# A two-layer decoder trunk on one core: in 17 groups of each mixed pass the fourth gathered row is summed on VectorE

## What is computed

```python
for layer in range(DEPTH):                       # 2
    h = rms_norm(x, norm_mix[layer])
    z = h @ w_in[layer]                          # 1024 x 2564
    ...
    mixed = jnp.concatenate([fox_o, dil_o, diff_o, s5_o], axis=-1)
    x = x + mixed @ w_out[layer]
    x = x + peer(rms_norm(x, norm_ffn[layer]), peer_wq[layer], peer_keys[layer],
                 peer_u[layer], peer_v[layer])
...
def chunk(xc):                                   # peer, 128 tokens
    ...
    ug = u_tab[ids]                              # ids: 128 tokens x 8 x 16
    act = gelu(einsum('td,thkd->thk', xc, ug)) * gate
    vg = v_tab[ids]
    return einsum('thk,thkd->td', act, vg)
```

## Time and profile before

| | before |
|---|---|
| median of 3 runs | 1836.35 us (1835.11 to 1844.07) |
| the profiled execution's own time | 1842.02 us |
| its span, first to last instruction | 1839.1 us |
| mean granted clock of PE | 0.905 of full speed |
| busy: PE / PEld | 1493.1 us (81%) / 799.9 us (43%) |
| busy: DVE / ACT / POOL | 1157.0 us (63%) / 389.9 us (21%) / 1082.8 us (59%) |
| moved by DMA | 649.87 MB, 353 GB/s on average |
| chain that ended last | PE 41%, DVE 32%, DMA 13%, issue 8%, POOL 4% |

### The profile page before, as it was taken

One profiled execution on the slowest core, in us unless ns is written; L12 is line 12 of the kernel. 1 busy time (PEld: TensorE's weight loads), 2 busy tenths in 40 slices (PEclk: granted clock), 3 DMA queues, 4 the chain that ended last, 5 costly groups with the idle time before them and its releaser, 6 DMA issues.

```text
span 1839.1 us, 15963 instructions
## 1 busy us (share of the span) xinstructions
PE 1493.1 (81%) x4780; PEld 799.9 (43%) x4780; DVE 1157.0 (63%) x2646; ACT 389.9 (21%) x991; POOL 1082.8 (59%) x1028
## 2 busy tenths in 40 slices
PE   6758379889898589889998579879998778777777
PEld 3546235445474234445464234445455433232332
DVE  6644954867469943877468933876648965445453
ACT  2221012233221121233221111233221121111111
POOL 0000345767666655777666655666766667777774
PEclk9768789989998889988999889999998988999889
DMA  7415589989999999999999999999999989999997
GB/s 307 160 35 207 204 359 380 399 297 363 373 401 408 340 418 409 405 369 385 374 401 408 336 415 351 395 340 331 374 376 405 369 301 410 409 409 409 407 388 307
DMA packets 179053, 649.87 MB, mean 353 GB/s; under 512 B 17783, under 2 KB 19319, under 8 KB 174105
## 3 DMA queue, kind: packets, MB, share of 16 engines
q0 software_dynamic: 147456, 536.94, 76.0%
q1 hardware_dynamic: 31512, 111.92, 15.7%
HBM read 644.07 MB, written 4.72 MB: 353 GB/s over the span
## 4 chain that ended last, share of the span: by engine, by line
PE 41%; DVE 32%; DMA 13%; issue 8%; POOL 4%; ACT 2%; DVEq 0%; SPq 0%; POOLq 0%
PE ps L1112 21%; DVE junk L865 12%; DMA ring_u<-table_u,ids 11%; PE ps L934 8%; PE ps L1069 3%; POOL ring_v L1143 2%; PE ps L1082 2%; DMA ring_v<-table_v,ids 1%; PE ps L999 1%; POOL ring_u L1138 1%; DVE W L690 1%; DVE W L842 1%; DVE W L844 1%; DVE W L845 1%; PE ps L1009 1%
## 5 line engine op out<-in xcount | busy, mean ns | idle before, releaser
L1112 PE MATMUL ps<-ring_v,diag 128*128 128x512 f32 x2048 | 982.4, 636 | 229.2 <-ACT diag L480 227.6
L865 DVE CUSTOM_DVE_ANT_0 junk<-ring_u,h 128x1024 bf16<-128x1024 f32 x512 | 627.4, 1225 | 268.1 <-DMA ring_u<-table_u,ids 212.5
L1138 POOL DMA_INDIRECT ring_u<-table_u,ids x512 | 536.1, 1047 | 387.7 <-DVE ids L849 204.9
L1143 POOL DMA_INDIRECT ring_v<-table_v,ids x512 | 546.5, 1067 | 352.2 <-PE ps L1112 269.9
L1112 PEld LDWEIGHTS ps<-ring_v,diag 128*128 128x128 f32 x2048 | 412.0, 205 | 761.4 <-issue 751.6
L471 ACT ACTIVATE acts<-dots 128x4 f32<-128x4 f32 x128 | 26.3, 205 | 998.6 <-DVE dots L865 998.6
L480 ACT ACTIVATE diag<-cst,weights 128x128 f32<-128x128 f32 x512 | 163.5, 390 | 39.2 <-DVE weights L874 39.0
L934 PE MATMUL ps<-W,hT 128*128 128x384 f32 (+2 forms) x384 | 142.9, 531 | 4.0 <-DVE hT L576 2.6
L1082 PE MATMUL ps<-hT,W 128*128 128x128 f32 x1024 | 117.7, 276 | 2.7 <-DVE hT L576 2.6
L1082 PEld LDWEIGHTS ps<-hT,W 128*128 128x128 f32 x1024 | 116.0, 192 | 3.8 <-DVE hT L576 3.8
L934 PEld LDWEIGHTS ps<-W,hT 128*128 128x128 f32 x384 | 73.7, 193 | 72.3 <-issue 36.9
(11 more groups left out here) (247 smaller groups left out, 1050.4 us busy)
## 6 DMA issues: line engine op xcount, KB each, us to landing
W<-w_in SPq DMA_DIRECT2D x32, 1282.0 KB, 15.2
W<-peer_wq SPq DMA_DIRECT2D x16, 2048.0 KB, 21.0
W<-w_out SPq DMA_DIRECT2D x4, 4096.0 KB, 19.5
ring_u<-table_u,ids POOLq DMA_INDIRECT x512, 7.8
ring_v<-table_v,ids POOLq DMA_INDIRECT x512, 7.7
W<-keys_t SPq DMA_DIRECT2D x4, 1024.0 KB, 8.3
zkv<-gain_mix SPq DMA_DIRECT2D x4, 512.0 KB, 16.0
toep<-ring_u SPq DMA_DIRECT2D x1, 2048.0 KB, 7.4
```

The costliest lines, as they stand in the source:

```text
L865: v.tensor_tensor_reduce(junk[:, :], ring_u[:, s, :], h[:, b, :], 1.0, 0.0, ALU.mult, ALU.add, dots[:, s:s + 1]).then_inc(dots_done, 1)
L1112: mm = pe.matmul(ps[:, c, :], diag[:, s, :], ring_v[:, s, c * 512:(c + 1) * 512], start=False, stop=False, skip_group_check=True)
L1138: gp.indirect_dma_start(ring_u[:, k % RING, :], None, table_u, bass.IndirectOffsetOnAxis(ap=ids[:, b, k:k + 1], axis=0)).then_inc(u_in[k % ...
L1143: gp.indirect_dma_start(ring_v[:, k % RING, :], None, table_v, bass.IndirectOffsetOnAxis(ap=ids[:, b, k:k + 1], axis=0)).then_inc(v_in[k % ...
```

## The change

`summed_on_vector(n, k)` picks slots: the fourth slot of a group, in the groups 1 to 5 and 8 to 19 of the passes 0 to 2, 51 slots in all. For those, DVE multiplies the v rows with the slot's weights and adds them to x, right behind the weights and ahead of the group's piece of the preparation; ACT writes no diagonal and PE makes no product for them, and the v gather that reuses such a slot waits for DVE instead of PE. The product with zeros at a pass's start is left out (the first product of a pass starts the sum), and the one with the identity at its end too; `gathered` now adds the PSUM sum to x instead of copying.

```diff
+def summed_on_vector(n, k):
+
+    i = k // RING_G
+    return n + 1 < PASSES and k % RING_G == RING_G - 1 and (1 <= i <= 5 or 8 <= i <= 19)
+
+def tensor_sums(t):
+
+    return sum(not summed_on_vector(k // SLOTS, k % SLOTS) for k in range(t))
...
@@ scalar, weigh
-                    a.wait_ge(v_used, RING_G * (m - 1))
-                for s in range(g * RING_G, (g + 1) * RING_G):
-                    a.activation(diag[:, s, :], ident, ACT.Copy, scale=weights[:, s:s + 1]).then_inc(diag_ready, 1)
+                    a.wait_ge(v_used, tensor_sums(RING_G * (m - 1)))
+                for j in range(RING_G):
+                    s = g * RING_G + j
+                    if not summed_on_vector(n, RING_G * i + j):
+                        a.activation(diag[:, s, :], ident, ACT.Copy, scale=weights[:, s:s + 1]).then_inc(diag_ready, 1)
@@ vector, weigh
                 v.tensor_tensor(weights[:, ss], acts[:, ss], gates[:, b, i * RING_G:(i + 1) * RING_G], ALU.mult)\
                     .then_inc(weights_done, 1)
+                for j in range(RING_G):
+                    s, k = g * RING_G + j, RING_G * i + j
+                    if summed_on_vector(n, k):
+                        v.wait_ge(weights_done, m + 1)
+                        v.wait_ge(v_in[s], 16 * (m // 2 + 1))
+                        v.scalar_tensor_tensor(out=x[:, b, :], in0=ring_v[:, s, :], scalar=weights[:, s:s + 1], in1=x[:, b, :],
+                                               op0=ALU.mult, op1=ALU.add).then_inc(v_summed, 1)
+                        v.wait_ge(v_summed, vector_sums(SLOTS * n + k + 1))
@@ vector, gathered
-                v.wait_ge(acc_ps, n + 1)
-                v.tensor_copy(x[:, n % NB, :], ps[:, 0:2, :].rearrange("p c n -> p (c n)")).then_inc(x_done, 1)
+                v.wait_ge(v_used, tensor_sums(SLOTS * (n + 1)))
+                b = n % NB
+                v.tensor_tensor(x[:, b, :], x[:, b, :], ps[:, 0:2, :].rearrange("p c n -> p (c n)"), ALU.add).then_inc(x_done, 1)
@@ tensor, add_rows
-                    for c in range(2):
-                        pe.matmul(ps[:, c, :], zero[:, :], x[:, b, c * 512:(c + 1) * 512], start=True, stop=False,
-                                  skip_group_check=True)
-                for j in range(RING_G):
-                    s = g * RING_G + j
-                    pe.wait_ge(v_in[s], 16 * (m // 2 + 1))
-                    pe.wait_ge(diag_ready, RING_G * m + j + 1)
+                for j in range(RING_G):
+                    s, k = g * RING_G + j, RING_G * i + j
+                    if summed_on_vector(n, k):
+                        continue
+                    pe.wait_ge(v_in[s], 16 * (m // 2 + 1))
+                    pe.wait_ge(diag_ready, tensor_sums(SLOTS * n + k + 1))
...
-                if i == HALVES - 1:
-                    for c in range(2):
-                        mm = pe.matmul(ps[:, c, :], ident, x[:, b, c * 512:(c + 1) * 512], start=False, stop=True,
-                                       skip_group_check=True)
-                    mm.then_inc(acc_ps, 1)
@@ gpsimd
-                            gp.wait_ge(v_used, SLOTS * n + k - RING + 1)
+                            old = SLOTS * n + k - RING
+                            if summed_on_vector(old // SLOTS, old % SLOTS):
+                                gp.wait_ge(v_summed, vector_sums(old + 1))
+                            else:
+                                gp.wait_ge(v_used, tensor_sums(old + 1))
```

More of the change, by code:

```diff
@@ L115, in join, with vector_sums @@
         self.eng.wait_ge(self.sem, self.n)
+def summed_on_vector(n, k):
[3 more added lines that the diff above has]
+    return sum(not summed_on_vector(k // SLOTS, k % SLOTS) for k in range(t))
+def vector_sums(t):
+    return t - tensor_sums(t)
 def plan_steps():
@@ L189, in trunk @@
         mags = sb("mags", [P, DEPTH, NJ])
-        zero = sb("zero", [P, P])
         ids = sb("ids", [P, NB, SLOTS], U32)
@@ L242, in trunk @@
         s5_in_done = [sem(f"s5_in_{n}") for n in range(DEPTH)]
-        toep_ready, toep_ps, toep_copied, zero_set = sem("toep_ready"), sem("toep_ps"), sem("toep_copied"), sem("zero_set")
+        toep_ready, toep_ps, toep_copied = sem("toep_ready"), sem("toep_ps"), sem("toep_copied")
         s5_tabled, s5_out, out_stored = sem("s5_tabled"), sem("s5_out"), sem("out_stored")
@@ L248, in trunk @@
             sem("dots_done"), sem("gelu_done"), sem("weights_done"), sem("diag_ready"), sem("v_used"))
-        acc_ps, x_done = sem("acc_ps"), sem("x_done")
+        v_summed, x_done = sem("v_summed"), sem("x_done")
         dve_step, act_step = sem("dve_step"), sem("act_step")
@@ L489, in _ @@
             step = Order(v, dve_step)
-            v.memset(zero[:, :], 0.0).then_inc(zero_set, 1)
             v.wait_ge(once_in, 64)
@@ L1095, in add_rows @@
             def add_rows(n, i):
-                m, g, b = HALVES * n + i, i % 2, n % NB
+                m, g = HALVES * n + i, i % 2
                 if i == 0:
@@ L1102, in add_rows @@
                         pe.wait_ge(s5_tabled, DEPTH)
-                        pe.wait_ge(zero_set, 1)
-                    for c in range(2):
-                        pe.matmul(ps[:, c, :], zero[:, :], x[:, b, c * 512:(c + 1) * 512], start=True, stop=False,
-                                  skip_group_check=True)
-                for j in range(RING_G):
-                    s = g * RING_G + j
-                    pe.wait_ge(v_in[s], 16 * (m // 2 + 1))
-                    pe.wait_ge(diag_ready, RING_G * m + j + 1)
-                    for c in range(2):
-                        mm = pe.matmul(ps[:, c, :], diag[:, s, :], ring_v[:, s, c * 512:(c + 1) * 512], start=False, stop=False,
-                                       skip_group_check=True)
-                    mm.then_inc(v_used, 1)
-                if i == HALVES - 1:
-                    for c in range(2):
-                        mm = pe.matmul(ps[:, c, :], ident, x[:, b, c * 512:(c + 1) * 512], start=False, stop=True,
-                                       skip_group_check=True)
-                    mm.then_inc(acc_ps, 1)
+                for j in range(RING_G):
[4 more added lines that the diff above has]
+                    pe.wait_ge(diag_ready, tensor_sums(SLOTS * n + k + 1))
+                    for c in range(2):
+                        mm = pe.matmul(ps[:, c, :], diag[:, s, :], ring_v[:, s, c * 512:(c + 1) * 512], start=(k == 0),
+                                       stop=(k == SLOTS - 1), skip_group_check=True)
+                    mm.then_inc(v_used, 1)
             walk({"lines": lines_out, "turned": turned, "rows": rows, "project": project, "s5 in": s5_inputs, "bu": bu, "keys": keys, "logits": logits,
```

2 lines of the change are left out of this document (1 added, 1 removed).

## The result

| | before | with the change |
|---|---|---|
| median (range), 9 runs each | 1836.35 us (1831.40 to 1844.07) | 1853.92 us (1848.12 to 1862.49) |
| the profiled execution's span | 1839.1 us | 1856.6 us |
| mean granted clock of PE | 0.905 | 0.882 |
| busy: PE / DVE | 1493.1 / 1157.0 us | 1416.4 / 1224.3 us |

The ratio is 1.0089, with a 95% interval of 1.0070 to 1.0109: slower by 0.9%, where 0.5% faster was forecast. PE lost 77 us of work, DVE gained 67, and the span grew by 17.5 us.

The account below looks back on a forecast made before the run. PE was taken to bound the projection groups, PE or DVE in turn from group 5 on, DMA second. Terms -8.1 - 1.8 - 1.7 + 2.5 = -9.1 us took 1836.35 to 1827.3 us; range 1812 to 1842.

Parts of the forecast that it names:

- part 4: Groups 9 to 14: sums delay DVE's path, +0.7 us over groups 9 and 10, +1.45 each for 11 to 14.
- part 5: Groups 15 to 19: shorter PE products against DVE's sums, group 17 at -1.1 us; in total -3.1 us a pass.
- part 1: Projection groups 1 to 4: each loses 4 of 16 products, 1.72 us, on never-idle PE; 6.9 us less per pass.
- part 3: Group 5, DVE-bound, +0.8 us; group 8's sum free in the first and third pass, +1.4 in the second.
- Part 2: Each sum on DVE costs 1.45 us: 1284 ns as the norm's operation, plus some 0.17 us for the weights' end.
- Part 7: Losses given back: 1 us for full DMA in the second pass, 0.5 us per pass for cold clock; together +2.5.
- rival 4: No change, the clock: three more cold starts per pass on the chain, 1.7 us each; 1841 us, chance 0.07.
- Part 6: Ends of passes: zero products gone before the third pass, -1.8 us; identity products gone at the kernel's end, -1.7 us.
- Rival 1: Slower: DVE's queue waits for late v rows in groups 9 to 18, mean 1 us a sum; 1854 us, chance 0.13.
- second leg: Gather issues on POOL, lengthened by sums, make rows late; without cover 49 us less 9, +40; chance 0.03.
- Rival 2: Larger gain: DVE's part in groups 9 to 14 is absorbed, 6.5 us per pass, half likelier; 1812 us, chance 0.18.
- rival 3: No change: DMA absorbs the projection's gain in the first and second pass; 1840 us, chance 0.12.

Follow-up runs that it names:

- experiment 1: The change with no slot summed on DVE, only the zero and identity products gone; 1840.56 us against 1839.61 for the kernel before, ratio 1.0009.
- experiment 5: The change with the 51 slots' products and diagonals left out and no DVE sums instead; 1879.07 us against 1897.44 for the kernel before, ratio 0.9910.
- experiment 6: The change cut to 24 sums (groups 1 to 3, 9, 14, 16 to 18), placed where DVE waits; 1869.74 us, ratio 0.9857 to the kernel before.
- Experiment 7: The change's 51 sums, from group 9 on each moved to where DVE waits for PE; 1872.92 us, ratio 0.9873 to the kernel before.

## Why the prediction was wrong

**What bounds the kernel** was read right: PE in the projection groups, DVE from group 5 on. The sign hung on sizes. The forecast was 9.1 us less, the span grew by 17.5. Of the 26.6 us between them 8.8 lie in part 4, 7.9 in the middle of part 5, 5.3 in part 1, 5.2 behind group 20 and 4.4 in the ends; what is left takes off some 5. The range, 1812 to 1842, missed the 1853.92 measured.

*Part 1, the projection groups,* was mis-sized: 6.9 us a pass were taken, 5.1 came. It counted four groups of products. The fourth does stand on the chain, at 1153.82, but behind it comes the S5 input on DVE, which had waited for PE only 0.67 us. So no more than 0.67 of its 1.72 us could count, and part 3 had already set that off against the sum of group 5. Three groups are left, 5.2 us, and both rows were at hand.

*Part 2, what a sum costs DVE,* was right: 1285 ns against 1284 of the row taken, and 1.2 to 1.5 us a group where nothing else moved.

*Part 3, groups 5 and 8,* was right: +3.8 predicted, +3.6 measured.

*Part 4, groups 9 to 14,* is the step that failed most. In the second pass it came out near the mark (6.3 us measured, 5.1 predicted). In the first and third it was short by 4.2 and 3.5 us. Turn and logits of groups 10 and 12 run 1.7 us longer in both passes because PE now stands idle for 2.2 to 2.5 us ahead of them, and in the first pass those of group 14 run 1.6 us longer; in the third pass groups 10 and 12 make up the 3.5 us. In the first, groups 12 and 14 took 3.2 of the 4.2 us and group 10 little. Part 7 had the clock in it, with 0.5 us a pass, on the ground of an idle time of 3.33 us, and rival 4 was marked down since most of the v products so hit have slack; neither looked at the logits, which DVE waits for.

*Part 5, groups 15 to 19,* failed in its middle. The products of group 15 gave their 1.7 us (1.7 to 2.3 measured) and 18 to 20 were right. But group 17, counted as -1.1, cost 0.7 to 1.4. The step that failed is "PE's products are shorter": fewer they were, but with the cold start behind 4.9 to 6.5 us of idle time they and the turn took 0.6 to 1.0 us longer than before. In the second pass the rest is a late v row, 1.23 us. With part 4 this makes the cold clock the term that was mis-sized most: 0.5 us a pass taken, about 5 us found in the first and third pass and 1 us in the second.

*Part 6, the ends,* was worth 3.5 us and measured nothing (experiment 1), though its profile alone, 6 to 8 us ahead of the one before in the last pass, would have looked like a success.

*Part 7, what is given back:* the row of DMA in the second pass was not needed (the projection gained 5.1 us there as elsewhere). What was missing is the query weights' load. That this load is issued only behind the second output product, 16.35 us ahead of its use, could be read in the trace before, and no term looked at it.

*The rivals.* Rival 1 gave nearly the measured time, 1854, but not by its mechanism: of the 44.3 us of waits for rows, 38 fell in groups 2 to 4, where they are hidden. Where it was to bite, in groups 9 to 18, it did so at two places of the second pass, groups 16 and 17 (2.03 and 1.23 us), and with 0.33 us in group 17 of the third; the stretch from 15 to 18 came out 2 us worse there than in the two other passes. So it holds for about 3 us of the 17.5, not for 18. Its second leg, longer issues on POOL, did happen (see the last section): 48 issues that began beside a sum took 22 us more than issues with DVE idle. No more waits for rows came of it than those named. Rival 4, the clock, was the right family: the mean fell from 0.905 to 0.882. It had a chance of 0.07, and its count, three more cold starts a pass on the chain at 1.7 us, is about what the first and third pass show: two sets of logits and the products of group 16. That it gave 1841 and not the measured time is owed to the other terms of the sum. Rival 2 was contradicted: in the second and third pass groups 11, 13 and 14 each grew by 1.2 to 1.5 us, about the sum's own 1.45. Its price did not follow from its terms either: with half of 20 us absorbed it would be 1817, not 1812. Of rival 3 nothing was seen.

What was argued and not shown: that leaving all 51 products out (experiment 5) gains less than the 24 well placed sums (experiment 6) because of the clock, 0.882 against 0.891; the intervals just touch. Experiment 7 speaks against the clock alone: it has the same 51 products gone and a mean clock as low (0.875), and with all the sums on DVE it came out no slower (0.9873). Why the query weights' load takes longer in the change wasn't tried, nor the change's sums with the load issued earlier. And why the change is 0.9% slower on one kind of chip and level on the other is open.

## What to carry to other kernels

Work moved from one engine to another is paid for by its place on the new queue as much as by its length: all 51 sums where the change has them cost 0.9% or nothing, and with those of groups 9 to 19 put behind what the other engine waits for the kernel gained 1.3%. So list for each group what the other engine waits for, issue that first, and put the moved work where the trace shows the receiving engine idle. Count relief only in the pieces whose next instruction on the relieved engine is on the chain, and where that engine's work gets shorter than its partner's, price the cold clock on the operations that the partner waits for.

## What was unexpected

- PE went to the low clock after idle times of 2.2 to 2.5 us (2.42, 2.21, 2.51, 2.31 us before L1048, clock 0.72 over the 6.1 us behind the first), not only after the 3.3 us of the earlier trace rows; in the second pass it stayed warm after 1.25 us. The length of the idle time does not settle it: in the kernel before, PE was idle for 3.87 us ahead of L1023 in group 14 of the first pass and of the third, and turn and logits ran at 1.00 in the one (4.11 us) and at 0.71 in the other (5.79 us).
- The averages of POOL's gather issues, 1061 and 1076 ns against 1047 and 1067, hide what the sums do to them. An issue that began while a sum was running ended 0.81 us after the sum's end, in 44 of 48 cases; these 48 took 1.40 us on average, against 0.94 us for issues with DVE idle. One of them, in group 15 of the third pass, with the sum ahead of it:

```profile
1305.98 1.28 DVE L897 SCALAR_TENSOR_TENSOR x<-ring_v,weights,x 128x1024 f32<-128x1024 f32 x1
...
1306.62 1.46 POOL L1156 DMA_INDIRECT ring_u<-table_u,ids  x1 [0.30 <-issue]
1308.38 0.93 POOL L1156 DMA_INDIRECT ring_u<-table_u,ids  x1 [0.30 <-issue]
```

  The rule that the prediction weighed from the Trainium skill, SBUF — State Buffer, section Who interferes with whom, is borne out by this: the issue is held up until the operation with two inputs in SBUF is done. The 51 sums raised POOL's busy time by only 11.8 us, since the time lost in the same way beside dots fell from 110 to 100 us.
- Chips differ more than the change does. Between 1600 and 1750 us, in the last pass, the rows of DMA rate read 397 GB/s for the change on the first chip and 369 on a later one, first and second fence:

```profile
1600.00:1750.00 150.00, 113.07 (x228) 46.16 (x226) 73.43 (x130) 20.75 (x70) 115.23 (x115) 0.91 1.01 397
```

```profile
1600.00:1750.00 150.00, 106.28 (x210) 43.63 (x211) 66.37 (x117) 20.43 (x69) 112.12 (x107) 0.90 0.98 369
```
